# First block's long convolutions and Fourier mixing dealt out between the later pairs of w_in, in three banks; attention's values one step later

## The reference, cut to what matters

```python
def long_conv(z, spec, d):
    n = z.shape[1]
    zf = z.astype(jnp.float32)
    y = jnp.fft.irfft(jnp.fft.rfft(zf, n=2 * n, axis=1) * spec[None], n=2 * n, axis=1)[:, :n]
    return (y + zf * d.astype(jnp.float32)).astype(z.dtype)

def hyena_mixer(u, sw, sb, spec, bias):
    u = short_conv(u, sw, sb)
    v, g1, g2 = jnp.split(u, HY_ORDER + 1, axis=-1)
    z = g1 * long_conv(v, spec[:, 0], bias[0])
    return g2 * long_conv(z, spec[:, 1], bias[1])

def fourier_mix(u):
    ...
    y = jnp.fft.fft2(ug, axes=(1, 3), norm='ortho').real
    ...
def mixer_sublayer(h, k_ext, v_ext, rope, w_in, ...):
    b, n, _ = h.shape
    p = h @ w_in
    ...
        att = block_attention(q, jnp.concatenate([k, k_ext], axis=1), jnp.concatenate([v, v_ext], axis=1))
    hy = hyena_mixer(p[..., OFF_HY:OFF_FN], sw, sb, spec, hy_bias)
    fn = fourier_mix(p[..., OFF_FN:OFF_GATE])
    return merge_branches(att, hy, fn, p[..., OFF_GATE:], w_branch, w_out), k, v
```

## Time and profile before

| | |
|---|---|
| median of 3 runs | 2709.72 us (2707.25 to 2710.53) |
| profiled execution | 2707.17 us, its span 2705.1 us |
| PE busy over the span | 2285.5 us (84%) |
| DVE, ACT busy | 822.3 us (30%), 394.8 us (15%) |
| `project_in`, first to last matmul | 58.2 to 206.5 us |
| `attention`, first matmul | 208.66 us |
| `hyena_fourier`, first matmul | 241.88 us |
| `project_out`, first matmul | 273.17 us |

### The profile page before, as it was taken

The page is one execution under the profiler, slowest core; times in us unless marked ns, Lnnn a source line. Parts: engine busy times, 40 slices in busy tenths (PEclk is TensorE's granted clock), DMA queues, the critical chain, the costliest instruction groups (busy, mean ns, idle before and its releaser), DMA issues. The chain is left out here.

```text
span 2705.1 us, 29323 instructions
## 1 busy us (share of the span) xinstructions
PE 2285.5 (84%) x12064; PEld 1580.6 (58%) x12064; DVE 822.3 (30%) x1566; ACT 394.8 (15%) x862; POOL 6.1 (0%) x11
## 2 busy tenths in 40 slices
PE   8997977655656665656899999999999999999998
PEld 5785742111112111111788886788888888678887
DVE  5725631000001000000543267431034415753001
ACT  2203020000000000000200145210010004441000
POOL 0000000000000000000000000000000000000000
PEclk9999979788887778888999999999999999999999
DMA  9542679999999999999986321086358833106430
GB/s 382 220 169 109 270 328 427 426 428 427 428 428 427 429 428 427 429 426 426 389 300 235 126 91 63 11 358 255 140 217 301 306 131 117 63 1 238 151 125 16
DMA packets 74908, 721.61 MB, mean 267 GB/s; under 512 B 8625, under 2 KB 11697, under 8 KB 13233
## 3 DMA queue, kind: packets, MB, share of 16 engines
q1 hardware_dynamic: 74800, 720.09, 66.0%
HBM read 719.01 MB, written 1.05 MB: 266 GB/s over the span
## 5 line engine op out<-in xcount | busy, mean ns | idle before, releaser
L1601 PE MATMUL bank<-pool 128*128 128x256 f32 x2720 | 596.7, 381 | 6.2 <-ACT pool L1528 6.2
L1601 PEld LDWEIGHTS bank<-pool 128*128 128x128 f32 x2720 | 516.7, 191 | 82.1 <-issue 12.3
L1192 PE MATMUL bank<-pool,moe_x_cur 128*32 128x512 f32 x1792 | 259.3, 714 | 141.1 <-DMA pool<-in_w_expert 140.8
L1633 PE MATMUL bank<-trunk_proj,pool 128*128 128x256 f32 x1408 | 306.4, 379 | 0.0
L1633 PEld LDWEIGHTS bank<-trunk_proj,pool 128*128 128x128 f32 x1408 | 266.6, 190 | 36.6 <-issue 0.8
L1192 PEld LDWEIGHTS bank<-pool,moe_x_cur 128*32 128x32 f32 x1792 | 54.1, 120 | 329.7 <-DMA pool<-in_w_expert 224.5
L1208 PE MATMUL bank<-pool,moe_hidT 128*32 128x512 f32 x896 | 153.5, 822 | 76.5 <-DMA pool<-in_w_expert 68.6
L1820 PE MATMUL bank<-pool 128*128 128x256 f32 x672 | 148.1, 380 | 0.0
L1360 DVE TENSOR_TENSOR moe_hid<-bank,moe_silu 128x512 f32<-128x512 f32 x16 | 11.1, 692 | 446.6 <-ACT moe_silu L1316 446.6
L1820 PEld LDWEIGHTS bank<-pool 128*128 128x128 f32 x672 | 127.3, 190 | 19.9 <-issue 2.6
L1208 PEld LDWEIGHTS bank<-pool,moe_hidT 128*32 128x32 f32 x896 | 29.1, 132 | 181.0 <-DMA pool<-in_w_expert 113.0
(11 more groups left out here) (586 smaller groups left out, 2164.7 us busy)
## 6 DMA issues: line engine op xcount, KB each, us to landing
pool<-in_w_expert SPq DMA_DIRECT2D x168, 2048.0 KB, 35.6
pool<-in_w_ff SPq DMA_DIRECT2D x132, 1024.0 KB, 7.0
pool<-in_w_ada SPq DMA_DIRECT2D x66, 1024.0 KB, 7.0
moe_more<-in_w_expert SPq DMA_DIRECT2D x24, 2048.0 KB, 35.9
pool<-in_w_in SPq DMA_DIRECT2D x40, 1024.0 KB, 4.8
pool<-in_w_mod SPq DMA_DIRECT2D x24, 1024.0 KB, 7.8
pool<-in_w_out SPq DMA_DIRECT2D x10, 1024.0 KB, 9.9
pool<-in_small SPq DMA_DIRECT2D x2, 2560.0 KB, 13.2
```

Source lines behind the costliest of these rows:

```text
L1192: mm = pe.matmul(ps[b][quarter[g], :], x_cur[:, u], w[:, b, g], start=u == 0, stop=u == up_panels - 1)
L1601: mm = pe.matmul(self.ps[p % 3][:, j * T:(j + 1) * T], w[:, j * KD + k], self.hT[:, k], start=k == 0, stop=k == KD - 1)
L1633: mm = pe.matmul(self.ps[3 + q % 2][:, 0:T], w, x[:, k], start=k == 0, stop=k == nk - 1)
```

## The change

The stage `hyena_fourier` is gone. Its work stands in `project_in`: PE's part between the pairs 8 to 17, VectorE's between the panels of `w_mod` from n = 8 on, ACT's behind pairs 15 and 16. The convolutions use three banks (6, 3 and 4) in place of five, two results to a bank; buffers move to rooms that are free by then (`kv_room` is the slot of the panel of keys and values). The fourth `tile_sum` goes behind pair 16, its `turn` behind pair 17, and the third and fourth tile of the modulation share one half of `acc`, so that the fourth can't start before the third is summed. In `attention` the values and the store of a pair of heads come one step later, its buffers lie behind the seventh slot, and SP issues the 7 early panels at its start.

```diff
--- before.py
+++ after.py
@@ attention @@
         with st.block() as block:
+            @block.sync
+            def _(sp):
+                for slot, src, sem in early:
+                    sp.dma_start(slot, src).then_inc(sem, 16)
...
-                for s in range(steps + 3):
+                for s in range(steps + 4):
                     if s < steps:
                         for u in both(s):
                             scores(u)
-                    if s >= 4 and s % 2 == 0:
-                        values((s - 4) // 2)
+                    if s >= 5 and s % 2:
+                        values((s - 5) // 2)
...
-                    if s >= 4 and s % 2 == 0:
-                        store((s - 4) // 2)
+                    if s >= 5 and s % 2:
+                        store((s - 5) // 2)
@@ LongConv @@
-    def __init__(self, sems, c, ps, bufs, cst, spec, n, z, bias, gate, out):
-        self.c, self.ps, self.cst, self.n, self.z, self.bias, self.gate, self.out = c, ps, cst, n, z, bias, gate, out
+    def __init__(self, sems, c, banks, bufs, cst, spec, n, z, bias, gate, out):
+        self.c, self.cst, self.n, self.z, self.bias, self.gate, self.out = c, cst, n, z, bias, gate, out
+        self.turn_bank = banks[0]
+        self.bank = lambda f: banks[1 + f % 2][:, f // 2 * T:(f // 2 + 1) * T]
+        self.back = lambda ch: banks[0][:, ch * T:(ch + 1) * T]
...
         for j, f in enumerate((0, 2, 1, 3)):
             for t in range(NT):
-                mm = pe.matmul(self.ps[1 + f][:, 0:T], self.cst["dft_signal"][:, t, f * P:(f + 1) * P],
+                mm = pe.matmul(self.bank(f), self.cst["dft_signal"][:, t, f * P:(f + 1) * P],
...
     def dve_gate(self, ve):
+        ve.wait_ge(self.inverse, 2 * self.n + 2)
         for ch in range(2):
-            ve.wait_ge(self.inverse, 2 * self.n + ch + 1)
-            ve.scalar_tensor_tensor(self.out[:, ch], self.z[:, ch], self.bias[:, ch:ch + 1], self.ps[ch][:, 0:T],
+            ve.scalar_tensor_tensor(self.out[:, ch], self.z[:, ch], self.bias[:, ch:ch + 1], self.back(ch),
                                     MUL, ADD).then_inc(self.gated, 1)
@@ project_in @@
         swapped, by_sin, by_cos, rotated = (st.sem("head_" + n) for n in ("swapped", "by_sin", "by_cos", "rotated"))
+        other_out, signed = st.sem("other_out"), st.sem("signed")
+        conv_sems = [st.sem("conv_" + n) for n in ("turned", "copied", "transformed", "products", "mixed", "inverse", "gated")]
+        conv_mixed, conv_gated = conv_sems[4], conv_sems[6]
+        centre, ahead, short, first_made, mid_out, second = (
+            st.sem(n) for n in ("centre", "ahead", "short", "first_made", "mid_out", "second"))
+        tall = lambda a, n: a.rearrange("p (k t) -> p k t", k=n)
+        kv_room = ring[:, KV_SLOT * BLK * P:(KV_SLOT + 1) * BLK * P]
+        u_conv, z_conv = tall(extra[:, 8 * T:14 * T], 6), tall(extra[:, 14 * T:16 * T], 2)
+        bufs = tall(extra[:, 4 * T:6 * T], NT), tall(kv_room[:, 0:4 * T], 4), tall(kv_room[:, 4 * T:8 * T], 4)
+        mid = kv_room[:, 4 * T:8 * T].rearrange("p (c t n) -> p c t n", c=2, t=NT)
+        v = lambda k, j=0, n=1: vec[:, V1[k][0] + j:V1[k][0] + j + n]
+        x_conv, x_fourier, hy_out, fn_out = proj[:, 4:10], proj[:, 10:12], spare[:, 4:6], spare[:, 6:8]
+        banks = ps[6], ps[3], ps[4]
+        conv = [LongConv(conv_sems, c, banks, bufs, branch, spec, 0, u_conv[:, 0:2], v("hy_bias", 0, 2), u_conv[:, 2:4], z_conv),
+                LongConv(conv_sems, c, banks, bufs, branch, spec, 1, z_conv, v("hy_bias", 2, 2), u_conv[:, 4:6], hy_out)]
...
-        sum_behind = {4: 0, 8: 1, 12: 2, 15: 3}
+        sum_behind = {4: 0, 8: 1, 12: 2, 16: 3}
+        acc_of = lambda tile: acc[:, (0, 1, 0, 0)[tile]]
...
+                def fourier_first():
+                    pe.wait_ge(conv_mixed, 2)
+                    for n, (ch, t) in enumerate((ch, t) for ch in range(2) for t in range(NT)):
+                        mm = pe.matmul(ps[3 + ch][:, t * T:(t + 1) * T], x_fourier[:, ch, t * P:(t + 1) * P],
+                                       branch["fn_channel"], start=True, stop=True)
+                        if t == NT - 1:
+                            mm.then_inc(first_made, 1)
+
+                def fourier_second():
+                    pe.wait_ge(mid_out, 2)
+                    for ch in range(2):
+                        for n, (t, part) in enumerate((t, part) for t in range(NT) for part in range(2)):
+                            mm = pe.matmul(ps[3][:, ch * T:(ch + 1) * T], mid[:, ch, t, part * P:(part + 1) * P],
+                                           branch["fn_token"][:, t, part * T:(part + 1) * T], start=n == 0, stop=n == 3)
+                    mm.then_inc(second, 1)
 
...
+                    if p == 8:
+                        pe.wait_ge(short, 2)
+                        pe.wait_ge(other_out, 1)
+                        conv[0].pe_turn(pe)
+                    if p == 9:
+                        pe.wait_ge(by_sin, 3)
+                        conv[0].pe_transform(pe)
+                    if p == 11:
+                        conv[0].pe_inverse(pe)
+                    if p == 12:
+                        pe.wait_ge(conv_gated, 4)
+                        conv[1].pe_turn(pe)
+                    if p == 13:
+                        conv[1].pe_transform(pe)
+                    if p == 15:
+                        conv[1].pe_inverse(pe)
+                        fourier_first()
+                    if p == 16:
+                        fourier_second()
...
-                        sc.activation(k_other, ps[6], ACT.Copy)
+                        sc.activation(k_other, ps[6], ACT.Copy).then_inc(other_out, 1)
+                    if p == 15:
+                        for ch in range(2):
+                            sc.wait_ge(first_made, ch + 1)
+                            sc.activation(mid[:, ch], ps[3 + ch].rearrange("p (t n) -> p t n", t=NT), ACT.Copy)\
+                                .then_inc(mid_out, 1)
+                    if p == 16:
+                        sc.wait_ge(second, 1)
+                        sc.activation(fn_out, ps[3].rearrange("p (c n) -> p c n", c=2), ACT.Copy)
...
-                            ve.wait_ge(sums_made, tile - 1)
-                        ve.tensor_scalar(acc[:, tile % 2], w[:, 0], cond[:, 0, 0:1], None, MUL)\
+                            ve.wait_ge(sums_made, (1, 3)[tile - 2])
+                        ve.tensor_scalar(acc_of(tile), w[:, 0], cond[:, 0, 0:1], None, MUL)\
                             .then_inc(mod_step, 1)
...
+                def short_conv(n):
+                    for j in (2 * n, 2 * n + 1):
+                        ve.tensor_scalar(u_conv[:, j], x_conv[:, j], v("short_w", 6 + j), v("short_b", j), MUL, ADD)\
+                            .then_inc(centre, 1)
+                    for j in (2 * n, 2 * n + 1):
+                        ve.wait_ge(centre, j + 1)
+                        ve.scalar_tensor_tensor(u_conv[:, j, 1:T], x_conv[:, j, 0:T - 1], v("short_w", j),
+                                                u_conv[:, j, 1:T], MUL, ADD).then_inc(ahead, 1)
+                    for j in (2 * n, 2 * n + 1):
+                        ve.wait_ge(ahead, j + 1)
+                        ve.scalar_tensor_tensor(u_conv[:, j, 0:T - 1], x_conv[:, j, 1:T], v("short_w", 12 + j),
+                                                u_conv[:, j, 0:T - 1], MUL, ADD).then_inc(short, 1)
+
                 for n in range(16):
+                    if n == 12:
+                        short_conv(2)
+                        ve.wait_ge(short, 4)
+                        conv[0].dve_gate(ve)
+                        conv[1].dve_copy(ve)
                     mod_panel(n)
                     if n == 2:
                         rotary.vector_angles(ve)
                     if n == 3:
-                        rotary.vector_signs(ve)
+                        rotary.vector_signs(ve).then_inc(signed, 1)
                         ve.wait_ge(consts_here, 16)
                     if 4 <= n < 7:
                         scale(n - 4)
                     if 6 <= n < 9:
                         rotate(n - 6)
+                    if n == 8:
+                        ve.wait_ge(signed, 1)
+                        ve.wait_ge(d.bank_free, 5)
+                        short_conv(0)
+                    if n == 10:
+                        ve.wait_ge(rotated, 3)
+                        conv[0].dve_copy(ve)
+                        short_conv(1)
+                    if n == 11:
+                        conv[0].dve_mix(ve)
+                    if n == 13:
+                        conv[1].dve_mix(ve)
                     if n % 4 == 3 and n > 4:
                         tile_add(n // 4 - 1)
+                ve.wait_ge(short, 6)
+                conv[1].dve_gate(ve)
                 tile_add(tiles - 1)
@@ hyena_fourier @@
-            @block.tensor
-            def _(pe):
```

(45 more changed lines are left out.)

79 lines of the change are left out of this document (18 added, 61 removed).

## The result

The changed kernel takes 2690.4 us (median of 4 runs, 2688.5 to 2692.13) against 2708.67 before (4 runs): ratio 0.9929, interval 0.9917 to 0.9941. The direction was right; the forecast of 2695.0 was 4.6 us too high, and the time lies 0.6 under the range's lower end of 2691. About 1 us of the 4.6 is the base: the kernel before measured 2708.67 here, and the forecast was worked out from 2709.72. The rest is in the gain, 18.3 us against the 14.5 of the sum.

What follows compares the result with a forecast made beforehand. PE bounds project_in; in attention and hyena_fourier no engine is full, and waits between engines leave gaps. -31.3 + 20.0 + 0.3 - 3.5 = -14.5 us gave 2692.7 against the profiled execution, 2695 for the median; range 2691 to 2701.

Steps and rivals of the forecast that it cites:

- the sum: Whole kernel up to project_out: -31.3 + 20.0 + 0.3 - 3.5 = -14.5 us.
- `project_in` pays PE's time and nothing else: In project_in: PE waits nowhere for VectorE, so the stage grows by PE's added 20.0 us.
- The end of the stage: End of project_in: fourth turn behind the last pair and more semaphores to clear; 0 to 0.8 us, 0.3 taken.
- The stage that goes: hyena_fourier, from its first matmul to project_out's, closing barrier included: all 31.29 us go.
- The loads: 7 early loads, moved to attention's start: cost nothing, since attention is longer than the stage hiding them now.
- Attention: Attention with values one step later: waits of 3.97 us gone, 0.5 for new ones, gain 3.5 us.
- The three waits: In attention, PE's waits for ACT's copies at values 0, 1 and 2: 0.61, 1.15 and 2.21 us, all gone.
- 241.88 - 208.66: Old attention's length, from its first matmul to hyena_fourier's; less 3.5 it leaves 29.7 us.
- the upper bound of 3.97: Attention's largest gain, 3.97 us, if no new wait comes.
- The rival that the clock would fall in the new attention: In attention: longer scores and transposes alone lower the clock; one fall costs 1.7 us, time 2697; chance 0.04.
- From there the same distances as before: From project_out's start at 258.5 to 259 on, everything later keeps its distances.
- the rival that the gain is given back later: Experts' stage, bound by DMA: earlier start lost if its loads don't start earlier; time 2709, no change; chance 0.05.

Runs made afterwards that it cites:

- packed: The changed kernel with each long convolution's transform directly behind its turn, no pair between them; 2697.05 us, ratio 0.9963.
- pad4: The changed kernel with 4 more matmuls behind project_in's last pair, into a bank nobody reads; 2689.87 us, ratio 0.9927.
- before_b1: The kernel before, unchanged, traced again; span 2708.5 us, attention 34.96 us.

## Why the prediction was right or wrong

**`project_in` pays PE's time and nothing else: right.** 20.0 + 0.3 forecast; 170.40 - 150.46 = 19.94 in the undisturbed traces. PE waited for none of the links, and packed shows that this hangs on the pairs between them: 2.53 us of wait where one is taken away. The end of the stage cost 0.16 of the 0.3 (PE idle for 2.37 us ahead of attention, 2.21 before), so PE's part was 19.8.

**The stage that goes: right, with one premise that doesn't hold.** 31.29 us in all four traces of the kernel before, the fall of the clock in it included. The loads were said to cost nothing because attention "is longer than the one that hides them now". It was (33.22 against 31.29), but the change makes it shorter, 29.39 us, as the prediction's own 29.7 says. It still covers them: `project_out`'s first matmul doesn't wait for them.

**Attention: the mechanism right, the size too small.** The three waits went; 0.5 was counted for new ones, and 0.20 came, with 0.05 more at the last values. Undisturbed it gives 3.8 and not 3.5. One step that failed is the price of the old attention, "241.88 - 208.66" with a clock of 1.00: that was the cheapest of four draws. With the clock's falls it is 34.5 on average, and the gain 4.8, above the upper bound of 3.97. With the draws of `project_in` (170.8 on average against 151.3, so 19.5 and not 20.3) the mixer gives 16.5 in place of 14.5. The rival that the clock would fall in the new attention, on the ground that transposes count for less than matmuls (the Trainium skill, "TensorE: Matmul & The Clock Gate", Part 4: PE-mode transpose), came true in one of the changed kernel's four traces; it fell more often in the old order, which had the same transposes and longer waits. No trace here separates the two.

**"From there the same distances as before": wrong, and the other step that failed, in the traces the larger one.** The sum ended at `project_out`. The experts kept their distance (1024.2 to 1025.4 us before, 1024.3 to 1024.7 after), so the rival that the gain is given back later fell: bound by DMA or not, their loads moved with the stage. But the second block was shorter by 3.3 us on average in the traces. About half of that is the clock's return 3 us behind its first matmul instead of 6, and the rest lies at the two shorter stretches at 0.50 later in it. This term wasn't in the sum at all, and no bound allowed for it: I let the clock act only where PE's work changed.

In the traces the parts add up to 16.5 + 3.3 = 19.8 us; the medians of the runs are 18.3, 17.4 and 18.0 us apart. The traces flatter the changed kernel: three of its four traced executions are the quickest of their groups (2688.5, 2689.96 and 2688.6, against medians of 2690.4, 2691.42 and 2691.8), while 2707.17 to 2711.36 for the kernel before lies around its medians. So some part is smaller in executions without a trace; whether the mixer's or the second block's, no run shows. How much of the measured 18.3 is the second block's stays open with it. Why four of four traces of each kernel stand on the same side stays open too: the traces show the block on either side with a shift ahead of it, not what brings each kernel there.

No version beat the changed kernel beyond the noise: pad4's ratio of 0.9927 lies within its interval.

## What to carry to other kernels

Work that ping-pongs between two engines cost only the busier engine's time here once its links were dealt out between pieces of a saturated stream, each gap long enough for the other engine's link; lay out the dates and look for the smallest margin. Before summing against one trace, take three or four of the kernel before: here a stage differed by 1.9 us between traces of the same program. And a change of some us upstream can go with another clock in a later stage that it doesn't touch, here one that begins behind 6 us of idle PE, so the range needs a few us for such stages.

## What the runs showed of the hardware

The granted clock's falls stood at different places in traces of the same kernel, also in attention, where PE's longest wait is 2.21 us: its clock was 1.00 there in the first trace and 0.90 in before_b1. With 0.34 us more ahead of a block that follows 6 us of idle PE, the half-speed stretch behind its first matmul was 5.5 and 6.1 us long instead of 2.8 to 3.0. Where that first stretch was 5.3 us or longer, two later ones in the block were longer as well, in all ten traces. And 2.9 us of added work on the path came out as no loss in the runs (ratios 1.0005 and 0.9988), with a block that was 6.5 and 2.7 us shorter in their traces.
